# Rotating the S5 states back on GpSimd, and expert weights in pieces of 1 MB

## The reference

```
proj = rmsnorm(h) @ w_in                    # q, k, v, r, a_low, u
o_gla = gla(q, k, v, gates)                 # gated linear attention in chunks
bu = einsum(B, u)                           # S5: complex diagonal state space,
h_t = ab * h_{t-1} + bu_t                   #   64 groups x 64 states, scan over the rows
y5 = Re(C h) + d_skip * u
h = h + concat(o_gla, glu(gelu(y5))) @ w_out
# MoE: 320 tokens, 32 experts, each token goes to 2 of one group of 8
h = h + sum_e weight_e * (silu(x @ w_gate[e]) * (x @ w_up[e])) @ w_down[e]
```

## Time and profile before

| | |
|---|---|
| median of three runs | 1714.49 us (1713.48 to 1716.72) |
| profiled execution | 1714.49 us, span 1712.7 us |
| TensorE busy | 1275.2 us (74%) |
| VectorE busy | 574.4 us (34%) |
| ScalarE busy | 193.8 us (11%) |
| GpSimd busy | 99.8 us (6%) |
| read from HBM | 478.29 MB |
| granted TensorE clock, mean | 0.879 |

### The profile page before, as it was taken

How to read it: one execution, slowest core, us unless ns; L and a number is a source line. 1 busy time by engine, 2 the same in 40 slices (tenths; PEclk the granted TensorE clock), 3 DMA queues, 4 the chain that set the end, 5 groups by cost and what they waited for, 6 DMA issues and landing times.

```text
span 1712.7 us, 21124 instructions
## 1 busy us (share of the span) xinstructions
PE 1275.2 (74%) x8701; PEld 737.6 (43%) x8701; DVE 574.4 (34%) x1029; ACT 193.8 (11%) x428; POOL 99.8 (6%) x250
## 2 busy tenths in 40 slices
PE   5999999999998999586575674655755755764747
PEld 4655555556766888373232322322323322322312
DVE  2199999983354000520120120210301201201214
ACT  3111111114212000200000000000000000000002
POOL 5910000000001000200000000000000000000000
PEclk9989999999999999787787797887978978877978
DMA  8331121224125972249999999999999999999995
GB/s 199 99 98 51 49 88 60 79 69 147 41 91 179 358 297 82 92 197 422 426 423 427 424 427 427 425 426 425 426 425 426 419 425 427 422 418 424 406 425 200
DMA packets 116299, 486.93 MB, mean 284 GB/s; under 512 B 18479, under 2 KB 81083, under 8 KB 81355
## 3 DMA queue, kind: packets, MB, share of 16 engines
q1 hardware_dynamic: 113344, 472.99, 69.5%
q0 software_dynamic: 2688, 12.97, 2.1%
q10 hardware_dynamic: 200, 0.02, 0.0%
HBM read 478.29 MB, written 10.78 MB: 286 GB/s over the span
## 4 chain that ended last, share of the span: by engine, by line
DMA 38%; PE 37%; DVE 14%; issue 4%; POOL 3%; SPq 2%; ACT 1%; DVEq 0%; POOLq 0%; ACTq 0%
DMA arena<-in_w_up 38%; PE ps L2000 10%; PE ps L1829 7%; PE ps L1861 7%; PE ps L1956 2%; PE ps L1865 2%; POOL arena L611 2%; PE ps L1778 2%; PE ps L1906 1%; DVE arena L1193 1%; DVE arena L1206 1%; PE ps L2036 1%; DVE arena L1179 1%; DVE arena L1180 1%; DVE arena L1207 1%
## 5 line engine op out<-in xcount | busy, mean ns | idle before, releaser
L2000 PE MATMUL ps<-arena 128*32 128x256 f32 x4096 | 335.9, 494 | 298.9 <-DMA arena<-in_w_up 297.8
L2000 PEld LDWEIGHTS ps<-arena 128*32 128x32 f32 x4096 | 174.0, 140 | 480.3 <-issue 448.7
L1829 PE MATMUL ps<-arena 128*128 128x336 f32 (+1 forms) x1152 | 341.4, 453 | 0.2 <-ACT arena L943 0.2
L1829 PEld LDWEIGHTS ps<-arena 128*128 128x128 f32 x1152 | 220.3, 195 | 115.9 <-issue 24.9
L1530 DVE COPY arena<-ps 128x256 f32<-128x256 f32 x31 | 13.0, 420 | 461.0 <-PE ps L2000 461.0
L2036 PE MATMUL ps<-arena 128*32 128x512 f32 x1024 | 121.8, 611 | 24.6 <-DVE arena L1537 19.5
L1513 DVE TENSOR_TENSOR arena<-arena,ps 128x1024 f32<-128x1024 f32 (+1 forms) x48 | 58.4, 1218 | 167.5 <-PE ps L1956 167.5
L1861 PE MATMUL ps<-arena 128*128 128x256 f32 x512 | 112.6, 381 | 0.4 <-issue 0.4
L1861 PEld LDWEIGHTS ps<-arena 128*128 128x128 f32 x512 | 96.6, 190 | 14.8 <-issue 2.0
L1956 PE MATMUL ps<-arena 128*128 128x512 f32 (+3 forms) x192 | 94.8, 616 | 6.2 <-DVE arena L1513 6.2
L2036 PEld LDWEIGHTS ps<-arena 128*32 128x32 f32 x1024 | 32.6, 111 | 95.9 <-issue 78.0
(11 more groups left out here) (342 smaller groups left out, 1028.0 us busy)
## 6 DMA issues: line engine op xcount, KB each, us to landing
arena<-in_w_gate SPq DMA_DIRECT2D x64, 2048.0 KB, 18.6
arena<-in_w_up SPq DMA_DIRECT2D x64, 2048.0 KB, 23.1
arena<-in_w_down SPq DMA_DIRECT2D x128, 1024.0 KB, 24.1
arena<-in_w_in SPq DMA_DIRECT2D x16, 2048.0 KB, 9.1
arena<-in_w_out SPq DMA_DIRECT2D x8, 2048.0 KB, 10.0
arena<-in_state_gla SPq DMA_DIRECT2D x8, 512.0 KB, 8.9
arena<-in_w_glu SPq DMA_DIRECT2D x4, 1024.0 KB, 5.0
out_new_gla_sample<-arena SPq DMA_DIRECT2D x2, 2048.0 KB, 24.7
```

Of the source, the lines that this page charges most:

```text
L1829: mm = te.matmul(o, w, x, start=(k == 0), stop=(k == kt - 1))
L2000: mm = te.matmul(ps[CAP * x:CAP * x + CAP, 0, 256 * (i % 2):256 * (i % 2) + 256], xT[:, 4 * q + k, CAP * i:CAP * i + CAP], wpiece[4 * (q / ...
```

## The change

Two edits. The program of `rotate_back` leaves VectorE's loop and stands, with the same waits and the same four operations, as a loop over j in GpSimd's program, behind the preparation. And the expert weights of gate and up are loaded by quarters: each piece has its own transfer of 1 MB with 8 KB a row, is waited for by itself, and is loaded again as soon as its q is over. The order of the pieces becomes gate, up, gate, up, one pair for each q.

```diff
@@ SP: expert_weights
-                        if j % 2:
-                            continue
-                        half, up = j // 4, j // 2 % 2
-                        src = A[("w_gate", "w_up")[up]][0].rearrange("e (p k) n -> e p (k n)", k=KT)
-                        src = src[bass.ds(e, 1), :, 4096 * half:4096 * half + 4096]
-                        dst, used = arena[:, 2048 * j:2048 * j + 4096], 4 * half + 4
+                        src = A[("w_gate", "w_up")[j % 2]][0].rearrange("e (p k) n -> e p (k n)", k=KT)
+                        src = src[bass.ds(e, 1), :, 2048 * (j // 2):2048 * (j // 2 + 1)]
                     else:
                         src = A["w_down"][0][bass.ds(e, 1), 128 * (j - 8):128 * (j - 7), :]
-                        dst, used = wpiece[j], j + 1
                     if first is not None:
-                        sp.wait_ge(weights_used, 12 * first + (used - 12))
-                    sp.dma_start(dst, src.rearrange("e p n -> (e p) n")).then_inc(piece_loaded[j], 16)
+                        sp.wait_ge(weights_used, 12 * first + j - 11)
+                    sp.dma_start(wpiece[j], src.rearrange("e p n -> (e p) n")).then_inc(piece_loaded[j], 16)
@@ GpSimd, behind masks_made, before memset(S)
+            for j in range(NJ):
+                c, q = j // 4, j % 4
+                cs, sn = (bc(E[c % 2][:, r_:r_ + 1, q, :], 1, 2) for r_ in range(2))
+                g_, q1 = Gs[j % 2], Q1[j % 2]
+                pool.wait_ge(scanned, 2 * (j + 1))
+                if j >= 2:
+                    pool.wait_ge(h_used, j - 1)
+                    pool.wait_ge(hl_saved, j - 1)
+                if j:
+                    pool.wait_ge(rotated, 2 * j)
+                st.sync()
+                mul(q1, cs, g_)
+                mul(Q2, sn, g_)
+                st.sync()
+                gp.tensor_tensor(q1[:, 0], q1[:, 0], Q2[:, 1], ALU.subtract).then_inc(rotated, 1)
+                gp.tensor_tensor(q1[:, 1], q1[:, 1], Q2[:, 0], ALU.add).then_inc(rotated, 1)
@@ VectorE
-            def rotate_back(j):
...
                 forward(j)
-                rotate_back(j)
@@ TensorE: expert, gate and up
-                    if q % 2 == 0:
-                        pe.wait_ge(piece_loaded[2 * q], 16 * (n + 1))
-                        pe.wait_ge(piece_loaded[2 * q + 2], 16 * (n + 1))
+                    pe.wait_ge(piece_loaded[2 * q], 16 * (n + 1))
+                    pe.wait_ge(piece_loaded[2 * q + 1], 16 * (n + 1))
@@
-                                           wpiece[4 * (q // 2) + 2 * (x // 2) + q % 2][:, HID * k + 256 * (x % 2):HID * k + 256 * (x % 2) + 256],
+                                           wpiece[2 * q + x // 2][:, HID * k + 256 * (x % 2):HID * k + 256 * (x % 2) + 256],
```

## The result

| | median, us | lowest to highest | ratio to before |
|---|---|---|---|
| before | 1715.24 | 1713.48 to 1716.72, 4 runs | |
| after | 1729.94 | 1727.35 to 1730.00, 4 runs | 1.0094, 95% interval 1.0079 to 1.0109 |

The changed kernel is 0.94% slower by the ratio (16.1 us); the medians lie 14.7 us apart. The profiled execution took 1730.94 with a span of 1729.0, against 1714.49 and 1712.7: 16.3 us more span. The forecast was 1745: the direction is right, the loss is about half of the 30 us that were forecast. The question behind it is which terms were too large.

A forecast was written before the change was run, and what follows sets the result against it. VectorE was taken to lead the S5 stage by 3.8 us a group, and transfers to bound the MoE stage. 1714.5 + 28 + 7 - 5 = 1744.5, forecast 1745 us, range 1704 to 1765.

The forecast's parts named there:

- Exclusion between GpSimd and two-input VectorE operations: S5 stage: GpSimd and VectorE operations reading two SBUF tiles shut each other out; 71%, own range 1718 to 1756.
- Rival (a): S5 stage: the engines don't disturb each other, TensorE's 33.6 us a group becomes the bound; 1696 us, 10%.
- Rival (b): S5 stage: the engines share by element, a rotate costing VectorE 2.7 us, a third under P1 and P2; 1703 us, 11%.
- Rival (c): S5 stage: VectorE's gapless operations starve GpSimd, TensorE and scans wait for rotated; +20 on top, 1765 and up, 8%.
- The term of +28: S5 stage: cost in us of moving the rotate back to GpSimd, over 28 j, bounds +2 and +39.
- lead-in of 0.16 us: Each GpSimd operation: 0.16 us at its start may hold nothing on VectorE, so a rotate holds 4.4 to 5.0 us.
- the +39: S5 stage: upper bound in us of the rotate's cost, if GpSimd holds VectorE off for the whole instruction.
- my main case: S5 stage: exclusion with one rotate of 5.0 us on GpSimd, holding VectorE off for 4.4 to 5.0 us.
- my own lower end: S5 stage: +24 us for the rotate's move, from 21 x 0.5 without tables plus 7 x 1.9 with tables.
- Costs put at nothing: S5 stage: other costs lie under cover, such as rotated(j) coming about 6 us after scan(j), not 2.5.
- The pieces: +7 forecast: MoE stage: 8 KB rows cost 0.12 us per 4 MB, 59 such steps, +7 us; bound below 0.
- The end: -5 forecast: Last expert: q 0 needs 2 MB less with quarters, so it starts 5 us earlier; bound above 0.

The follow-up runs named there:

- the kernel that only writes: Kernel before, rotate left out; GpSimd instead fills the same tiles with zeros, reading no SBUF: 1694.15 us, ratio 0.9858.
- The two half moves: Kernel before with the rotate on GpSimd only for the 25 j not beside tables (1717.13 us), or only for the 7 j beside them (1726.89 us).
- the kernel that does this alone: Kernel before with quarters of 1 MB for the last expert only, halves of 2 MB elsewhere: 1712.77 us, ratio 0.9979.
- rows of 8 KB: Kernel before, still with transfers of 2 MB, but each row written as two pieces of 8 KB: 1725.80 us, ratio 1.0050.
- 25 of them, placed well: Kernel before with one rotate product on GpSimd for 25 j, VectorE doing the next j's P1 and P2 first: 1696.05 us, ratio 0.9879.

## Why the prediction was right in direction and wrong in size

**Exclusion between GpSimd and two-input VectorE operations: right.** P1 and P2 stay at 0.85 us, the adds and table products that meet a GpSimd operation with reads get longer, and with the reads taken away they don't. Rival (a) (no disturbance, 1696) falls for this kernel, but the kernel that only writes shows that its price for a VectorE set free was good (-21 forecast, -20.7 measured at the first expert). Rival (b), sharing by element, falls too: it gave 2.7 us held for one rotate, and beside the tables it was 4.03. Rival (c), starving, is not there: GpSimd gets its turn after each VectorE instruction, even beside the tables.

**The term of +28 is the step that failed, by its size: it measured +12.** Its lead-in of 0.16 us was good: a product of 1.6 us holds a table product for 2.75 - 1.28 = 1.47 and 2.70 - 1.28 = 1.42, nearly the whole instruction and not all of it, as the +39 would have it. The sums were too dear: taken as 0.90 long, 0.74 held, they hold a table product for 1.87 - 1.29 = 0.58 each. So one rotate holds VectorE 4.03 us, less than the 4.4 at the low end of my main case, and 4.03 - 2.51 = +1.5 beside the tables (forecast +1.9 to +2.6). Without tables, by the same rows, 1.36 + 0.70 + 0.58 = 2.64 us stay outside P1 and P2 (the three operations of the slice at 324.40 less their own 0.51, 0.50, 0.19), against 2.51 saved: +0.13, not +0.5 to +1.0. One slice in each group is shorter again, 6.97, because GpSimd starts 0.27 us before P1 there (315.44 against 315.71), beside the reading of y, which has a PSUM input. The account from my own lower end: 24 less 28 x 0.37 for the shorter hold, less 7 x 0.31 for that slice, 24 - 10.4 - 2.2 = 11.4, measured 12.2. The rest of the miss is that I took 28 out of 24 to 39, although the cheaper rows of the same group (0.75 for the sum) were there.

**Where the loss sits.** The forecast gave the 21 j without tables about half of it. The two half moves put all of it beside the seven tables (+11.5 of 12.3). What decides is not GpSimd's time but what VectorE does meanwhile.

**Costs put at nothing: right.** The late rotate does not hold TensorE up: its weight loads of L1722 wait 4.2 us in all for it, 0.5 at most, and its matmuls not at all in after. The last scan and the release of w_down are both 12.2 us late, but that they agree is luck of the clock, as said above. Gain at the start 0: quarters go out at 754.92, yet w_down is released as late as the rest.

**The pieces: +7 forecast, +9 measured.** Row size was the right cause, and it was small by a fifth: 0.14 to 0.16 us for 4 MB, not 0.12; 30 x 0.3 = 9.

**The end: -5 forecast, -4.8 measured** in the kernel that does this alone. In after, 30 x 0.3 - 4.8 = 4.2 would be due from the release of w_down to the last start, and 3.2 were measured, and 3.4 with quarters alone, so it is not chance; where this 1 us comes from was not followed. The 0.7 us of slow clock behind it was not in the forecast.

**Sum.** 12.2 + 3.2 + 0.7 = 16.1, against 16.3 in the spans.

**What one profile can tell.** Between the last scan and the release of w_down kernels with the same front part differ: 769.15 before, 771.72 with quarters alone, 773.72 with rows of 8 KB, and 785.67 with the rotate on GpSimd alone, where after has 781.32. The traces say where this arises: the same groups of matmuls take their longer or their shorter time in different places. The long block of 64 records takes 19.18 us before and 17.49 with quarters alone (from 402 to 407 us granted 0.66 and 1.00); it starts 0.4 us later than before with quarters alone, 2.1 later with rows of 8 KB and 1.0 earlier with quarters for the last expert, though all of these have the same program up to there. So a difference of 2 to 4 us at one milestone of one execution need not be an effect of the change. What sets the places was not tried.

## What to carry to other kernels

Before work goes from VectorE to GpSimd, list what VectorE does at that moment: here GpSimd's time was free beside instructions with a PSUM input, and beside those with two SBUF inputs VectorE paid nearly all of it, so move only as much as fits under the former, and move nothing beside the rest. The full move of 128 instructions lost 0.8%, and 25 of them, placed well, gained 1.2%. Compare two kernels at the engine that is the bound: the last scan came 30.6 us earlier in one kernel, and TensorE only 20.6. In a stage that runs at the rate of the transfers keep the rows long, and cut transfers small only where something waits for the first bytes: here at the last expert.

## What the runs showed that was not expected

- GpSimd and VectorE hand over after each single instruction: beside 1.28 us products of VectorE, GpSimd's pair of 3.19 us stretches to 4.23 and its sums from 1.04 and 1.16 to 1.83 and 1.94, and neither engine starves.
- The held time is counted as busy on both engines. VectorE's busy time rose from 574.4 to 582.2 us with 128 instructions fewer; only the durations by shape show it.
- Rows of 8 KB against 16 KB cost about 1.5% of the transfer rate (9.94 to 9.95 us for 4 MB against 9.80), in transfers of 2 MB as of 1 MB.
